# Up projections of the last feed-forward as seven block products instead of eight, in a two-block transformer kernel

## The chip, the cores and the metric

The kernel runs on one core of one Trainium2 chip. The metric is device time in microseconds, median of the runs. TensorE (PE) multiplies matrices: the weights are loaded as the stationary operand (PEld), the activations stream past them, and products accumulate in PSUM, a memory of eight banks of 512 float32 columns, here two tensors `acc` and `sco` of four banks each. VectorE (DVE), ScalarE (ACT) and GpSimd (POOL) do elementwise work; all three reach SBUF, the on-chip memory that holds every other tensor here. SyncE (SP) issues the DMA loads of the weights.

## The reference

Two transformer blocks run one after the other on 512 tokens with 1024 features. The second block adds 16 meta tokens and is feed-forward, attention mixers, feed-forward. Only the last feed-forward changes:

```
def rms_norm(x, g):
    xf = x.astype(jnp.float32)
    y = xf * lax.rsqrt(jnp.mean(xf * xf, axis=-1, keepdims=True) + EPS)
    return (y * g.astype(jnp.float32)).astype(x.dtype)

def swiglu(x, w_in, w_out):
    g, u = jnp.split(x @ w_in, 2, axis=-1)
    return (jax.nn.silu(g) * u) @ w_out

h = h + token_mixer(rms_norm(h, norm_mix[l]), ...)
h = h + 0.5 * swiglu(rms_norm(h, norm_ffn2[l]), w_ffn2_in[l], w_ffn2_out[l])
return rms_norm(h, final_norm)[:, N_META:]
```

`w_ffn2_in` is 1024 x 5632 (gate half and value half of 2816 columns each), `w_ffn2_out` is 2816 x 1024. All inputs are float32.

## The kernel before

Tensors lie transposed: features on the 128 partitions, tokens along the row. A feature axis of 1024 is 8 tiles of 128 rows. Every product is made from two roundings, `x = x_hi + x_lo` and `w = w_hi + w_lo`, each part in the rounded float32 that PE takes in one pass, as three matmuls: `w_hi x_hi + w_hi x_lo + w_lo x_hi`.

The program is a list of phases (`PHASES`). The change touches three of them. `("proj_out", 2)` is the output projection of the mixers, which also adds to `h`, forms `xn_hi` and `xn_lo` (the input of the feed-forward times its gain) and lets POOL sum the squares of `h` for the norm. `("up", 3, 0)` and `("up", 3, 1)` compute gate and value for 11 tiles of hidden features each (22 in all), and `("down", 3, 0)` and `("down", 3, 1)` project those 11 tiles back.

A turn of an up phase makes one tile of hidden features. It is two items: item 0 is the gate tile, item 1 the value tile, in weight slots 0 and 1 (`raw0`, `raw1`). An item is 8 input tiles by 3 matmuls, that is 24 matmuls of 128x512, with its weights handled in two halves of four tiles. For each item SP loads 512 KB in two DMAs, ACT rounds `raw` to `w_hi` (`split_hi`, line 1710), DVE subtracts to `w_lo` (`split_lo`, line 2272) and PE multiplies (`item`, line 1169). Then DVE multiplies the result in PSUM by `rstd` (line 2826), ACT takes the silu (line 2197), DVE multiplies gate by value (line 2862), ACT rounds the product to `hid_hi` (line 2200) and DVE subtracts to `hid_lo` (line 2869). POOL does nothing in these phases. The norm's factor `rstd` comes in the first turn from a matmul of the summed squares (line 1190), a root on ACT and a reciprocal on DVE (line 2811).

Order on each engine is program order. Engines meet through counting semaphores: `n.at(name, k)` is the count that a name has reached after k events of the present turn.

Of the kernel before, what the change touches and what calls it, by code (L numbers as in the profile page):

```python
# [133 lines left out]
UNSCALED = {("proj_out", 1): GAIN["norm_ffn_g"], ("down", 1, 1): N_VEC, ("proj_out", 2): GAIN["norm_ffn2_2"]}  # L134

# [401 lines left out]
def events(phase):  # L537
# [27 lines left out]
    if kind in ("proj_out", "down"):  # L565
        e = {**items(1, 1), **({"sq_ready": 2, "sq_added": 2} if sums_squares(phase) else {})}
        if phase in UNSCALED:
            e.update({"xhi_ready": 2, "xn_ready": 2})
        if phase == ("down", 1, 1):
# [3 lines left out]
        return 4, e  # L573
    if kind == "up":
# [23 lines left out]
class Tally:  # L598
# [19 lines left out]

    def loop(self, first, last, body):
# [29 lines left out]
def build(nc, A, out):  # L649
    with ExitStack() as ctx:  # L650
# [12 lines left out]
        merged = sb("merged", [P, KT, T])  # L663
# [20 lines left out]
        stats = sb("stats", [P, 44])  # L684
        eye, turn_a, turn_b = const[:, 0:P], const[:, P:2 * P], const[0:96, 2 * P:2 * P + 96]
# [39 lines left out]
        meta_tok = flat(probs[:, :, :])[0:META, 0:D]  # L725

# [164 lines left out]
        def _(sp):  # L891
# [90 lines left out]
            for index, ph in enumerate(PHASES):  # L982
# [44 lines left out]
                elif kind == "proj_out":  # L1027
# [4 lines left out]
                    n.loop(1, 4, turn)  # L1032
                elif kind == "up":
# [29 lines left out]
        def _(pool):  # L1063
# [89 lines left out]
        def _(pe):  # L1153
# [25 lines left out]
            def sums(number):  # L1179
# [461 lines left out]
            for index, ph in enumerate(PHASES):  # L1641
# [60 lines left out]
        def _(act):  # L1702
            n = Tally(act)

            def split_hi(slot, k, tiles):

                act.wait_ge(S[f"raw_in{slot}"], n.at(f"raw_in{slot}", 32 * k))
                act.wait_ge(S[f"item_done{slot}"], n.at(f"item_done{slot}", k - 1))
                for a, b, parts in split_parts(tiles):
                    act.activation(w_hi[slot][:, a:b, :], raw[slot][:, a:b, :], ACT.Copy).then_inc(  # L1710
                        S[f"hi_ready{slot}"], parts)

# [359 lines left out]
            for index, ph in enumerate(PHASES):  # L2072
# [137 lines left out]
        def _(dve):  # L2210
# [55 lines left out]
            def split_lo(slot, k, tiles):  # L2266

                done = 2 * k - 2
                for a, b, parts in split_parts(tiles):
# [3 lines left out]
                                      w_hi[slot][:, a:b, :].bitcast(F32), ALU.subtract).then_inc(S[f"split{slot}"], parts)  # L2273

# [456 lines left out]
            for index, ph in enumerate(PHASES):  # L2731
# [31 lines left out]
                elif kind == "resplit":  # L2763
                    c0 = META
                    for k in range(KT):
# [3 lines left out]
                                          ALU.subtract).then_inc(S["xn_ready"], 1)  # L2769
                elif kind in ("proj_out", "down"):  # L2770
# [3 lines left out]
                    def turn(i, tiles=own):  # L2774
                        for s in range(2):
# [129 lines left out]
```

## Time and profile before

| | |
|---|---|
| time, median of 3 runs | 2275.52 us (2275.37 to 2279.98) |
| profiled execution, span from first to last instruction | 2277.5 us |
| PE busy | 2219.2 us (97%) |
| DVE busy | 1243.9 us (55%) |
| ACT busy | 903.5 us (40%) |
| POOL busy | 220.5 us (10%) |
| mean granted clock of PE, share of full speed | 0.995 |

The profiled execution has no time of its own beside its span, which lies 2.0 us above the median of the timed runs and within their range. Busy times are sums over instructions; a busy PE includes overlap of pipelined matmuls.

### The profile page before, as it was taken

To read this page: it belongs to the slowest core of one execution; us is meant where nothing else is said; L and a number is where in the kernel's file an instruction comes from. 1 tells how busy PE (TensorE), PEld (TensorE's weight loads), DVE (VectorE), ACT (ScalarE), POOL (GpSimd) and SP (SyncE) were. 2 spreads that over 40 slices of the span, in tenths; PEclk is the share of its full clock that TensorE was granted. 3 is DMA by queue.
4 is the path that set the end of the run, shared out by engine and by line. 5 is a ranking of instruction groups with operands and counts; after the bars stand their busy time and mean duration, and the time that the engine had idled before them with its cause. 6 is when DMAs were issued, how large, how long until landed. Compare 5 with 4: busy or idle time off the path is not lost.

```text
span 2277.5 us, 36049 instructions
## 1 busy us (share of the span) xinstructions
PE 2219.2 (97%) x12592; PEld 1820.2 (80%) x12592; DVE 1243.9 (55%) x2668; ACT 903.5 (40%) x1815; POOL 220.5 (10%) x201
## 2 busy tenths in 40 slices
PE   8999999999999999999999899999999999999998
PEld 6567766778888889999999777777777787888887
DVE  5779786467736745533442545544555655443442
ACT  5455445444414443322322444444444433322332
POOL 0100043310000031000001000111100130000001
PEclk9999999999999999999999999999999999999999
DMA  4111211235533342342233222243333233332332
GB/s 119 36 37 37 65 47 52 79 102 150 157 102 95 113 129 78 91 129 88 85 106 99 57 85 81 74 111 94 98 92 98 81 97 89 95 108 77 97 105 75
DMA packets 400393, 205.67 MB, mean 90 GB/s; under 512 B 68956, under 2 KB 393928, under 8 KB 400284
## 3 DMA queue, kind: packets, MB, share of 16 engines
q1 hardware_dynamic: 399365, 203.83, 31.3%
q8 instruction: 63, 1.03, 0.2%
q10 hardware_dynamic: 919, 0.43, 0.1%
q14 instruction: 46, 0.38, 0.1%
HBM read 201.94 MB, written 14.80 MB: 95 GB/s over the span
## 4 chain that ended last, share of the span: by engine, by line
PE 64%; issue 19%; DVE 4%; ACT 2%; POOL 1%; POOLq 0%; DVEq 0%; ACTq 0%
PE acc L1169 34%; PE acc L1474 16%; PE acc L1220 5%; PE sco L1509 2%; PE acc L1573 1%; PE acc L1569 1%; DVE w_lo L2272 1%; PE sco L1262 1%; PE sco L1549 1%; POOL vT L1095 1%; PE acc L1309 1%; PE acc L1549 0%; PE sco L1529 0%; PE acc L1296 0%; DVE bias L2260 0%
## 5 line engine op out<-in xcount | busy, mean ns | idle before, releaser
L1710 ACT ACTIVATE w_hi<-raw 128x512 fp32r<-128x512 f32 (+4 forms) x656 | 372.0, 614 | 694.4 <-PE acc L1169 661.2
L2272 DVE TENSOR_TENSOR w_lo<-raw,w_hi 128x512 fp32r<-128x512 f32 (+4 forms) x656 | 423.2, 685 | 143.8 <-ACT w_hi L1710 139.5
L1169 PE MATMUL acc<-xn_hi,w_hi 128*128 128x512 f32 (+1 forms) x1408 | 421.1, 340 | 2.1 <-DVE qbuf L2826 2.1
L1169 PE MATMUL acc<-xn_lo,w_hi 128*128 128x512 f32 (+1 forms) x1408 | 422.1, 340 | 0.0
L1169 PE MATMUL acc<-xn_hi,w_lo 128*128 128x512 f32 (+1 forms) x1408 | 420.3, 339 | 0.0
L1169 PEld LDWEIGHTS acc<-xn_hi,w_hi 128*128 128x128 f32 x1408 | 241.9, 188 | 35.8 <-DVE qbuf L2826 3.0
L1169 PEld LDWEIGHTS acc<-xn_lo,w_hi 128*128 128x128 f32 x1408 | 241.2, 188 | 31.2 <-issue 0.5
L1169 PEld LDWEIGHTS acc<-xn_hi,w_lo 128*128 128x128 f32 x1408 | 241.5, 188 | 30.0
L1169 PE MATMUL acc<-hid_lo,w_hi 128*128 128x512 f32 (+1 forms) x832 | 261.5, 349 | 0.0
L1169 PE MATMUL acc<-hid_hi,w_lo 128*128 128x512 f32 (+1 forms) x832 | 260.6, 348 | 0.0
L1169 PE MATMUL acc<-hid_hi,w_hi 128*128 128x512 f32 (+1 forms) x832 | 259.8, 347 | 0.8 <-DVE hid_lo L2768 0.8
L2826 DVE TENSOR_TENSOR qbuf<-acc,v_tok 128x512 f32<-128x512 f32 (+1 forms) x132 | 91.7, 695 | 249.8 <-PE acc L1169 249.7
L1474 PE MATMUL acc<-xn_hi,w_hi 128*128 128x264 f32 (+1 forms) x576 | 187.7, 367 | 13.2 <-DVE xn_lo L2299 3.8
L2778 DVE SCALAR_TENSOR_TENSOR h<-acc,h 128x512 f32 (+3 forms) x64 | 44.5, 695 | 267.6 <-PE acc L1169 267.6
L1474 PE MATMUL acc<-xn_hi,w_lo 128*128 128x264 f32 (+1 forms) x576 | 172.8, 341 | 0.0
L1474 PE MATMUL acc<-xn_lo,w_hi 128*128 128x264 f32 (+1 forms) x576 | 172.5, 340 | 0.0
L1169 PEld LDWEIGHTS acc<-hid_hi,w_hi 128*128 128x128 f32 x832 | 144.5, 188 | 23.2 <-issue 1.1
L1169 PEld LDWEIGHTS acc<-hid_lo,w_hi 128*128 128x128 f32 x832 | 144.5, 188 | 21.2
L1169 PEld LDWEIGHTS acc<-hid_hi,w_lo 128*128 128x128 f32 x832 | 144.8, 188 | 20.4
L1474 PEld LDWEIGHTS acc<-xn_hi,w_hi 128*128 128x128 f32 x576 | 98.7, 189 | 36.8 <-issue 17.8
L1220 PE MATMUL acc<-xn_hi,w_hi 128*128 128x512 f32 x240 | 118.6, 494 | 0.9 <-DVE w_lo L2272 0.6
L1474 PEld LDWEIGHTS acc<-xn_hi,w_lo 128*128 128x128 f32 x576 | 99.3, 189 | 12.6
(397 smaller groups left out, 3065.7 us busy)
## 6 DMA issues: line engine op xcount, KB each, us to landing
raw<-in_w_ffn_in SPq DMA_DIRECT2D x176, 256.0 KB, 3.0
raw<-in_w_in SPq DMA_DIRECT2D x118, 256.0 KB, 3.2
raw<-in_w_up SPq DMA_DIRECT2D x88, 256.0 KB, 3.0
raw<-in_w_ffn_out SPq DMA_DIRECT2D x32, 384.0 KB, 3.3
raw<-in_w_gate SPq DMA_DIRECT2D x48, 256.0 KB, 3.0
raw<-in_w_ffn_out SPq DMA_DIRECT2D x32, 320.0 KB, 3.7
raw<-in_w_out SPq DMA_DIRECT2D x32, 256.0 KB, 2.8
bias<-grids_dram SPq DMA_DIRECT2D x64, 128.0 KB, 2.9
```

The lines of the kernel that those rows point to most:

```text
L1095: ins = pool.tensor_tensor(square_sum[:, c0:T], square_sum[:, c0:T], probs[:, s, c0:T], ALU.add)
L1169: mm = pe.matmul(acc[0:m, 2 * slot + b, 0:size], w[slot][:, t, 0:m], x[:, place(t), c:c + size], start=(t == 0 and w is w_hi and x is xh), ...
L1220: mm = pe.matmul(acc[0:m, slot, 0:SEQ], w[slot][:, t, 0:m], x[:, t, META:T], start=(t == 0 and w is w_hi and x is xh), stop=(t == tiles - ...
L1262: mm = pe.matmul(sco[:, hh, :], queries_a[i][r, P * (t - 1):P * t], kbuf[r, i // 2, META:T], start=True, stop=True)
L1309: mm = pe.matmul(acc[64 * hh:64 * hh + 64, 3, o:o + P], front_values(u)[:, 1 + b, 0:64], pt[:, hh, 1 + b, :], start=b == 0, stop=b == 3)
L1474: mm = pe.matmul(acc[:, b if wide else slot, 0:size], w[slot][:, t, :], x[:, t, c:c + size], start=(t == 0 and w is w_hi and x is xh), sto ...
L1509: mm = pe.matmul(sco[:, bank, to:to + size], qbuf[r, i % 2, TILES[t][0]:TILES[t][0] + P], kbuf[r, keys_at(name, i), c:c + size], start=Tru ...
L1549: mm = pe.transpose(turned_of[x % 2][:, b * P:(b + 1) * P], prob_of[u % 4][:, real + b * P:real + (b + 1) * P], eye)
L1710: act.activation(w_hi[slot][:, a:b, :], raw[slot][:, a:b, :], ACT.Copy).then_inc(S[f"hi_ready{slot}"], parts)
L2272: dve.tensor_tensor(w_lo[slot][:, a:b, :], raw[slot][:, a:b, :], w_hi[slot][:, a:b, :].bitcast(F32), ALU.subtract).then_inc(S[f"split{slot ...
L2778: dve.scalar_tensor_tensor(out=x, in0=banks(acc, 2 * s, blk), scalar=factor, in1=x, op0=ALU.mult, op1=ALU.add).then_inc(S[f"acc_free{s}"], 1)
L2826: dve.tensor_tensor(span(scaled[s], blk), banks(acc, 2 * s, blk), span(rstd, blk), ALU.mult).then_inc(S[f"acc_free{s}"], 1)
```

## The change

Each turn of the two up phases of the last feed-forward (`PAIRED = (3,)`) becomes one 2x2 block product by the scheme of Strassen and Winograd. The weights of a turn are four blocks of four input tiles each: even and odd input tiles, of the gate (a11, a12) and of the value. The activations are four blocks too: even and odd input tiles, left and right half of the tokens. Seven products of sums of blocks stand for the eight block products that gate and value need. Each product is 4 tiles by 3 matmuls of 128x256, so a turn is 84 matmuls of 256 columns in place of 48 matmuls of 512.

The weight sums `s1` to `s4` are made on POOL from the raw weights (`sum_blocks`), for the turn after the present one. ACT rounds seven blocks in each turn (`block_rounded`) and DVE lowers seven (`block_lowered`), each of 128x512. The sums of activation blocks (`t1` to `t4`) are made once, on POOL, in `("proj_out", 2)` (`feed`), and rounded and lowered there by ACT and DVE (`feed_pairs`).

Products accumulate in four banks of `sco`. Where one partial result serves two outputs, ACT copies it to SBUF (`copies`, in `kbuf`). DVE adds a bank and a copy (`joined`) for three of the four half tiles, POOL adds two copies for the fourth (`join_value`). DVE scales the gate by `rstd` and POOL the value (`scale_value`). Raw weights have two buffers: even turns use `aux`, odd turns `raw0` and `raw1`. The loads of a turn are four DMAs of 256 KB. The proj_out and up phases of this feed-forward are written out straight instead of in loops.

Core of the diff:

```diff
+PAIRED = (3,)
+PRODUCTS = ("a11", "a12", "s2", "s1", "s3", "a22", "s4")
@@ SP
+                    def pair_rows(r):
+                        ...
+                        sp.wait_ge(S["block_split"], n.at("block_split", -7 if r >= 2 else -7 * r))
+                        for s in range(2):
+                            c = (ph[2] * HALF + r) * P + s * D_FF
+                            for first in (0, 4):
+                                sp.dma_start(pair_raw[r % 2][s][:, first:first + 4, :],
+                                             w_up[ph[1]][:, first:first + 4, c:c + P]).then_inc(
+                                                 S[f"{landings(r)[0]}{s}"], 16)
@@ POOL
+            def sum_blocks(r, ahead):
+                ...
+                pool.wait_ge(S["block_split"], max(0, n.at("block_split", 7 * ahead - 3)))
+                pool.tensor_tensor(s_sums["s1"], value[:, 0], value[:, 1], ALU.add).then_inc(S["s_made"], 1)
+                pool.wait_ge(S["s_made"], n.at("s_made", done + 1))
+                pool.tensor_tensor(s_sums["s2"], s_sums["s1"], gate[:, 0], ALU.subtract).then_inc(S["s_made"], 1)
+                pool.tensor_tensor(value[:, 0], gate[:, 0], value[:, 0], ALU.subtract).then_inc(S["s_made"], 1)
+                pool.wait_ge(S["s_made"], n.at("s_made", done + 2))
+                pool.wait_ge(S["block_split"], n.at("block_split", 7 * ahead))
+                pool.tensor_tensor(s_sums["s4"], gate[:, 1], s_sums["s2"], ALU.subtract).then_inc(S["s_made"], 1)
+                    def pool_turn(r):
+                        if r > 0:
+                            scale_value(r - 1)
+                        if r + 1 < HALF:
+                            sum_blocks(r + 1, 1)
+                        join_value(r)
@@ PE
+                banks_of = (0, 1, 0, 2, 0, 3, 2)
+                for b, name in enumerate(PRODUCTS):
+                    pe.wait_ge(S["block_split"], n.of("block_split", r, b + 1))
+                    ...
+                    elif name == "s2":
+                        pe.wait_ge(S["copied"], n.of("copied", r, 1))
+                    elif name == "s1":
+                        pe.wait_ge(S["joined"], n.of("joined", r, 0))
+                    ...
+                    for j in range(4):
+                        ...
+                        for w, x in ((block_hi, x_hi), (block_hi, x_lo), (block_lo, x_hi)):
+                            mm = pe.matmul(sco[:, banks_of[b], 0:half], w[b][:, j, :], x,
+                            ...
@@ ACT
+                block_rounded(6, r, 0)
+                if r > 0:
+                    silu(r - 1)
+                copy(0, 0, 1)
+                next_block(0)
+                if r > 0:
+                    round_hidden(r - 1)
+                next_block(1)
+                copy(1, 0, 3)
+                next_block(2)
+                copy(2, 2, 4)
+                next_block(3)
+                copy(3, 0, 5)
+                next_block(4)
+                ...
+                next_block(5)
@@ DVE
+                if r > 0:
+                    gate_joined(r - 1)
+                    if r == 1 and ph[2] == 0:
+                        dve.wait_ge(S["root_ready"], n.of("root_ready", 0, 1))
+                        dve.reciprocal(rstd[:, first:T], root[:, first:T]).then_inc(S["rstd_ready"], 1)
+                        ...
+                    scale_gate(r - 1)
+                block_lowered(5, r, 0)
+                block_lowered(6, r, 0)
+                if r > 0:
+                    hidden(r - 1)
+                ...
+                dve.tensor_tensor(scaled[0][:, left], bank(1), copies[0][:, 0:half], ALU.add).then_inc(S["joined"], 1)
+                next_block(0)
+                if r > 0:
+                    lower_hidden(r - 1)
+                next_block(1)
+                next_block(2)
+                next_block(3)
+                next_block(4)
+                ...
+                dve.tensor_tensor(scaled[1][:, left], bank(3), copies[3][:, 0:half], ALU.add).then_inc(S["joined"], 1)
```

On DVE, one turn in the middle of the first up phase stands so in the kernel before (the lines 2271, 2856 and 621 are loop bookkeeping):

```order
L2826 TENSOR_TENSOR qbuf<-acc,v_tok 128x512
L2271 ISA
L2272 TENSOR_TENSOR w_lo<-raw,w_hi 128x512
L2271 REGISTER_ALU
L2272 TENSOR_TENSOR w_lo<-raw,w_hi 128x512
L2826 TENSOR_TENSOR qbuf<-acc,v_tok 128x512
L2272 TENSOR_TENSOR w_lo<-raw,w_hi 128x512 x2
L2856 REGISTER_ALU
L2862 TENSOR_TENSOR pt<-vT,qbuf 128x512
L2869 TENSOR_TENSOR hid_lo<-pt,hid_hi 128x512
```

and an even turn so in the changed kernel (`sco` is PSUM, all other names are SBUF; `kbuf` holds the copies, `wx` and `w` the seven rounded blocks):

```order
L2629 TENSOR_TENSOR qbuf<-sco,kbuf 128x256
L2634 TENSOR_TENSOR qbuf<-qbuf,v_tok 128x512
L2613 TENSOR_TENSOR w_lo<-aux,w_hi 128x512 x2
L2641 TENSOR_TENSOR pt<-vT,qbuf 128x512
L2668 TENSOR_TENSOR qbuf<-sco,kbuf 128x256
L2613 TENSOR_TENSOR wx_lo<-raw,wx_hi 128x512
L2647 TENSOR_TENSOR hid_lo<-pt,hid_hi 128x512
L2613 TENSOR_TENSOR wx_lo<-raw,wx_hi 128x512
L2613 TENSOR_TENSOR wx_lo<-aux,wx_hi 128x512
L2613 TENSOR_TENSOR w_lo<-aux,w_hi 128x512
L2613 TENSOR_TENSOR w_lo<-raw,w_hi 128x512
L2678 TENSOR_TENSOR qbuf<-sco,kbuf 128x256
```

A turn goes from 8 DVE instructions, six of them with both inputs in SBUF, to 13, ten of them with both inputs in SBUF.

On POOL, where nothing stood in these phases, a turn is now (two turns shown, the first with its sums from `raw`, the second from `aux`):

```order
L1188 TENSOR_TENSOR qbuf<-qbuf,v_tok 128x512
L1169 TENSOR_TENSOR aux<-raw1 128x512
L1171 TENSOR_TENSOR aux<-aux,raw0 128x512
L1172 TENSOR_TENSOR raw1<-raw0,raw1 128x4x128
L1175 TENSOR_TENSOR aux<-raw0,aux 128x512
L1196 TENSOR_TENSOR qbuf<-kbuf 128x256
L1188 TENSOR_TENSOR qbuf<-qbuf,v_tok 128x512
L1169 TENSOR_TENSOR aux<-aux 128x512
L1171 TENSOR_TENSOR aux<-aux 128x512
L1172 TENSOR_TENSOR aux<-aux 128x4x128
L1175 TENSOR_TENSOR aux<-aux 128x512
L1196 TENSOR_TENSOR qbuf<-kbuf 128x256
```

That is five instructions of 512 columns and one of 256 for each turn, all reading SBUF.

On DVE at the end of the output projection and the first turn of the up phase, the changed kernel has (line 2701 adds an item to `h`, 2613 lowers weight blocks, 2711 and 2696 lower activations and their sums):

```order
L2701 SCALAR_TENSOR_TENSOR h<-acc,h 128x512
L2613 TENSOR_TENSOR wx_lo<-aux,wx_hi 128x512 x3
L2613 TENSOR_TENSOR w_lo<-aux,w_hi 128x512 x2
L2711 TENSOR_TENSOR xn_lo<-qbuf,xn_hi 128x256
L2696 TENSOR_TENSOR xn_lo<-kbuf,xn_hi 128x256
L2701 SCALAR_TENSOR_TENSOR h<-acc,h 128x512
L2711 TENSOR_TENSOR xn_lo<-qbuf,xn_hi 128x512
L2696 TENSOR_TENSOR t_lo<-kbuf,t_hi 128x256 x3
```

Five weight blocks now stand ahead of the lowering of the last two activation tiles.

## Rows read from the trace of the kernel before

**Rows 1.** The page: busy time of each engine, and the chain that ended last
```profile
PE 2219.2 (97%) x12592; PEld 1820.2 (80%) x12592; DVE 1243.9 (55%) x2668; ACT 903.5 (40%) x1815; POOL 220.5 (10%) x201
PE 64%; issue 19%; DVE 4%; ACT 2%; POOL 1%; POOLq 0%; DVEq 0%; ACTq 0%
```

**Rows 2.** Windows: a 264-column phase, then the two last up phases
```profile
core 0: us, PE busy (x) PEld busy (x) DVE busy (x) ACT busy (x) POOL busy (x), PEclk, DMA share, GB/s
1065.33:1182.79 117.46, 117.46 (x962) 117.46 (x961) 52.85 (x80) 34.88 (x60) 0.00 (x0) 1.00 0.32 93
1914.49:2014.57 100.08, 100.08 (x433) 81.14 (x432) 47.12 (x73) 31.15 (x54) 0.00 (x0) 1.00 0.33 97
2092.47:2192.55 100.08, 100.08 (x433) 81.14 (x432) 47.13 (x72) 31.14 (x54) 0.00 (x0) 1.00 0.33 95
```

**Rows 3.** Groups by line, from 1600 us on: one instruction's mean ns
```profile
L2272 DVE TENSOR_TENSOR w_lo<-raw,w_hi 128x512 fp32r<-128x512 f32 x140 | 90.4, 687 | 29.4 <-ACT w_hi L1710 28.7
L2272 DVE TENSOR_TENSOR w_lo<-raw,w_hi 128x256 fp32r<-128x256 f32 x40 | 15.6, 429 | 16.8 <-ACT w_hi L1710 16.8
L1710 ACT ACTIVATE w_hi<-raw 128x512 fp32r<-128x512 f32 x140 | 80.5, 623 | 165.0 <-PE acc L1169 161.3 <-PE acc L1474 3.7
L1710 ACT ACTIVATE w_hi<-raw 128x256 fp32r<-128x256 f32 x40 | 14.3, 408 | 12.0 <-PE acc L1474 12.0
L2826 DVE TENSOR_TENSOR qbuf<-acc,v_tok 128x512 f32<-128x512 f32 x44 | 30.3, 691 | 104.5 <-PE acc L1169 104.5
L2862 DVE TENSOR_TENSOR pt<-vT,qbuf 128x512 f32<-128x512 f32 x22 | 15.0, 683 | 0.0
L2197 ACT ACTIVATE vT<-qbuf 128x512 f32<-128x512 f32 x22 | 13.6, 617 | 2.8 <-DVE qbuf L2826 2.8
```

**Rows 4.** Timeline of POOL (start, duration; both in us)
```profile
1426.24 1.50 POOL L1143 TENSOR_TENSOR bias<-bias,const 128x512 f32<-128x512 f32 x1
1435.99 1.09 POOL L1143 TENSOR_TENSOR bias<-bias,const 128x512 f32<-128x512 f32 x1
1701.32 1.29 POOL L1149 TENSOR_TENSOR merged<-merged,bias 128x512 f32<-128x512 f32 x1 [61.50 <-DVE small L2572]
1828.75 1.75 POOL L1149 TENSOR_TENSOR merged<-merged,bias 128x512 f32<-128x512 f32 x1 [9.82 <-DVE small L2572]
1845.51 2.27 POOL L1149 TENSOR_TENSOR merged<-merged,aux 128x512 f32<-128x512 f32 x1 [1.04 <-DVE small L2572]
1863.97 1.36 POOL L1095 TENSOR_TENSOR vT<-vT,probs 128x512 f32<-128x512 f32 x1 [4.87 <-ACT probs L2139]
```

**Rows 5.** Timeline of DVE around the same moments
```profile
1426.11 2.18 DVE L2272 TENSOR_TENSOR w_lo<-raw,w_hi 128x512 fp32r<-128x512 f32 x2
1701.28 0.50 DVE L2601 CUSTOM_DVE_ANT_0 aux<-sco,bias,small 128x272 f32<-128x272 f32 x1
1828.60 0.74 DVE L2272 TENSOR_TENSOR w_lo<-raw,w_hi 128x256 fp32r<-128x256 f32 x2
1845.36 1.27 DVE L2272 TENSOR_TENSOR w_lo<-raw,w_hi 128x512 fp32r<-128x512 f32 x2
1857.34 1.28 DVE L2272 TENSOR_TENSOR w_lo<-raw,w_hi 128x512 fp32r<-128x512 f32 x2
1859.09 0.75 DVE L2785 SCALAR_TENSOR_TENSOR xn_lo<-h,gains,xn_hi  x1 [0.46 <-ACT xn_hi L2147]
1864.68 1.20 DVE L2785 SCALAR_TENSOR_TENSOR xn_lo<-h,gains,xn_hi  x1 [0.50 <-ACT xn_hi L2147]
```

**Rows 6.** Timelines at the start of the up phase, DVE then PE
```profile
1904.45 3.35 DVE L2811 RECIPROCAL v_tok<-vT 128x512 f32<-128x512 f32 x1 [1.31 <-ACT vT L2177]
1907.84 1.29 DVE L2826 TENSOR_TENSOR qbuf<-acc,v_tok 128x512 f32<-128x512 f32 x2
...
1908.59 0.50 PE L1169 MATMUL acc<-xn_hi,w_hi 128*128 128x512 f32 x1 [1.07 <-DVE qbuf L2826]
```

**Rows 7.** The page's DMA issues: KB each, us to landing
```profile
raw<-in_w_ffn_in SPq DMA_DIRECT2D x176, 256.0 KB, 3.0
```

**Rows 8.** Windows (columns as in the second group): the first 60 us
```profile
0.00:60.00 60.00, 50.61 (x231) 38.84 (x231) 36.95 (x72) 32.83 (x61) 4.93 (x14) 0.91 0.43 119
```

More of the change, by code:

```diff
@@ L573, in events @@
         return 4, e
+    if paired(phase):
+        return HALF, {"s_made": 4, "block_hi": 7, "block_split": 7, "product": 7,
+                      "copied": 4, "joined": 3, "value_half": 1, "gate_scaled": 1, "value_scaled": 1, "hid_hi": 1, "hid_ready": 1,
+                      "silu_ready": 1, "hid_ready_f32": 1}
     if kind == "up":
@@ L617, in at, with of @@
         return self.turn * self.each.get(event, 0) + (self.before.get(event, 0) + k)
+    def of(self, event, turn, k):
+        return self.before.get(event, 0) + turn * self.each.get(event, 0) + k
     def loop(self, first, last, body):
@@ L1073, in _ @@
                 pool.memset(raw[s][:, :, :], 0.0).then_inc(fills, 1)
+            def sum_blocks(r, ahead):
+                done = 4 * ahead
+                gate, value = (even_odd(x) for x in pair_raw[r % 2])
+                kind, landed = landings(r)
+                for s in range(2):
+                    pool.wait_ge(S[f"{kind}{s}"], n.at(f"{kind}{s}", landed))
+                pool.wait_ge(S["block_split"], max(0, n.at("block_split", 7 * ahead - 3)))
[6 more added lines that the diff above has]
+                pool.tensor_tensor(s_sums["s4"], gate[:, 1], s_sums["s2"], ALU.subtract).then_inc(S["s_made"], 1)
@@ L1074, in _, with scale_value, join_value @@
             for index, ph in enumerate(PHASES):
                 n.enter(index)
-                if sums_squares(ph):
+                if paired(ph):
+                    first, last = (META, T) if columns_of(ph) == 1 else (0, T)
+                    def scale_value(r):
+                        pool.wait_ge(S["joined"], n.of("joined", r, 2))
+                        pool.wait_ge(S["value_half"], n.of("value_half", r, 1))
+                        if r == 0:
+                            pool.wait_ge(S["rstd_ready"], n.of("rstd_ready", 0, 1 if ph[2] == 0 else 0))
+                        pool.tensor_tensor(scaled[1][:, first:last], scaled[1][:, first:last], rstd[:, first:last],
+                                           ALU.mult).then_inc(S["value_scaled"], 1)
+                    def join_value(r):
+                        half = (T - first) // 2
+                        pool.wait_ge(S["copied"], n.of("copied", r, 4))
+                        pool.wait_ge(S["hid_ready_f32"], n.of("hid_ready_f32", r, 0))
+                        pool.tensor_tensor(scaled[1][:, first + half:T], copies[2][:, 0:half], copies[3][:, 0:half],
+                                           ALU.add).then_inc(S["value_half"], 1)
+                    def pool_turn(r):
[4 more added lines that the diff above has]
+                        join_value(r)
+                    for r in range(HALF):
+                        n.straight(r, pool_turn)
+                    scale_value(HALF - 1)
@@ L1672, in _ @@
                     final()
+                elif paired(ph):
+                    for r in range(HALF):
+                        n.straight(r, lambda i: pairs(ph, i))
                 elif kind in ("proj_out", "up", "down"):
@@ L1711, in split_hi, with block_rounded @@
                         S[f"hi_ready{slot}"], parts)
+            def block_rounded(j, r, ahead):
+                (kind, landed), name = landings(r), PRODUCTS[j]
+                if name in ("a11", "a12"):
+                    act.wait_ge(S[f"{kind}0"], n.at(f"{kind}0", landed))
+                elif name == "a22":
+                    act.wait_ge(S[f"{kind}1"], n.at(f"{kind}1", landed))
+                else:
+                    act.wait_ge(S["s_made"], n.at("s_made", 4 * ahead + {"s1": 1, "s2": 2, "s3": 3, "s4": 4}[name]))
+                act.activation(block_hi[j], block_source(name, r), ACT.Copy).then_inc(S["block_hi"], 1)
@@ L2774, in turn @@
                     def turn(i, tiles=own):
+                        if tiles == (0, 0) and index + 1 < len(PHASES) and paired(PHASES[index + 1]):
+                            for j in range(5):
+                                block_lowered(j, 0, 0)
                         for s in range(2):
```

273 lines of the change are left out of this document (267 added, 6 removed).

## The prediction

> **What bounds the kernel now.** The page comes first: PE is busy 97% of the span, the chain that ended last is mostly PE and issue, and POOL is busy 10% [rows 1]. Then the windows over the two up phases: 100.08 us hold 18 items of 24 matmuls, all of it PE busy at full clock, DVE busy 47.12, ACT 31.15, POOL 0 [rows 2]. So an item takes 100.08 / 18 = 5.56 us, a turn of two items 11.12 us, the 22 turns 244.6 us. Nothing but PE matters there. Last the groups and the timelines of DVE and POOL, for what the added instructions cost. The runs' median is 2275.5 us and the profiled span 2277.5; I add the sum to the span and take 2 us off at the end.
>
> **What PE gains.** 48 matmuls of 512 columns become 84 of 256. A 512-column matmul takes 5.56 / 24 = 231.7 ns. The 264-column phase has 962 in 117.46 us, 122.1 ns each, with its weight loads busy without a gap [rows 2]. A line through both gives 0.442 ns a column and 5.4 ns, so 118.6 ns at 256 columns: 84 x 118.6 = 9.96 us a turn. If the weight load is what holds 264 columns at 122.1, it is 10.26. I take 9.96. If PE stayed the bound: 22 x (11.12 - 9.96) = 25.5 us gained.
>
> **What ACT and the loads cost: nothing.** ACT gets seven roundings, 0.62 each, four copies of 256 columns at 0.41, silu 0.62, and a hidden rounding like it [rows 3]: 7.2 us under a turn of 10 or more. Loads stay 1 MB a turn in 256 KB pieces, 3.0 us to landing [rows 7]; a raw buffer is free after the seventh block of turn r-2, a quarter into that turn, and is read a turn later, some 8 us. Uncovered, a late load would delay `s1` and all behind it.
>
> **What DVE and POOL cost by themselves.** DVE has ten instructions of 512 columns and three of 256 with one input in PSUM. At 0.69 and 0.43 [rows 3] that is 8.2 us, back to back less (a pair takes 1.28, so the second adds 0.60 [rows 5]). POOL has five of 512 and one of 256: an undisturbed one takes 1.29 [rows 4], half for the small one, 7.1 us. Each alone fits under 9.96.
>
> **But not side by side.** This is the step that decides. The rows pair up in time:
> - DVE lowers two blocks from 1845.36 to 1846.63 [rows 5]. POOL's sum starts at 1845.51 and ends at 1847.78, 2.27 us against 1.29 undisturbed, 1.15 after DVE ends [rows 4]. At 1828.75 it takes 1.75 and ends 1.16 after DVE.
> - The other way: DVE's `xn_lo` takes 0.75 at 1859.09, and 1.20 at 1864.68 under POOL's 1863.97 to 1865.33; it ends 0.55 after POOL [rows 4, 5].
> - At 1426 both meet: DVE's pair takes 2.18 for 1.28, POOL 1.50 for 1.09.
> - A DVE instruction with one input in PSUM and one in SBUF, at 1701.28, leaves POOL's at 1.29.
>
> So a DVE instruction with two SBUF inputs and a POOL one that reads SBUF hardly overlap. The Trainium skill, "SBUF — State Buffer", section "Who interferes with whom", has this rule: DVE's second SBUF input goes through a read interface that GpSimd shares, and the later one fully blocks. The direction agrees with the rows; its size is a rival below.
>
> Ten of DVE's thirteen and all six of POOL's are of that kind. The floor of a turn is then 10 x 0.60 + 5 x 1.15 + 0.60 (the small one: bounds 0.58 from half of 1.15 and 0.65 from half of 1.29) = 12.35 us, above PE's 9.96 and above the 11.12 of today. Bounds: if the sums, whose inputs are strided, run like the mask addition (1.09 alone; 1426 to 1428.29 is 2.18 for three instructions, so 2.18 - 1.20 = 0.98 for POOL's), four of them at 0.98 give 11.65. If each handover costs what an undisturbed start does, 10 x 0.69 + 5 x 1.29 + 0.65 = 14.0.
>
> **Does the order fill it?** I laid out one turn. DVE's gate join runs beside POOL's `scale_value`; then scaling, two lowerings and `hidden` run as a train while POOL's `s1` stands; `s1` goes in the left join's place; lowering 0, `lower_hidden` and lowering 1 run; now DVE has nothing until `s2` is summed and rounded, so POOL runs `s2` and `s3`; then lowering 2 and 3, POOL's `s4` while ACT rounds `s3`, lowering 4, the value join, with `join_value` behind it. The interface is in use nearly all the time and the layout closes at 12.45. PE's seven products have two and a half us of slack in it: `s2` waits for copy 0, that for the silu, that for the scaled gate. I take **12.5** (nearer 12.35 than 14.0, since DVE's instructions come in trains and an alternation ends 0.55, not 0.69, after POOL).
>
> **The edges.** Turn 0 has no scaling or hidden work (seven lowerings and five POOL instructions, 9.4 us on the interface, with waits 10.5). Turn 10 has no sums and no next blocks: PE's 9.96, with the wait for the gate 10.3. Its tail (join, scale, silu, hidden, roundings, some 5 us) is hidden by down's first item, which reads the last hidden tile after 10 tiles of 3 matmuls, 6.95 us. A phase is 10.5 + 9 x 12.5 + 10.3 = 133.3 us against 122.3: +11.0, twice is +22.0.
>
> At the start of the first phase, let E be the end of the last output item. POOL reaches `sum_blocks(0)` only behind the activation sums and squares of the item pair before, about E - 4.5, so `s1` to `s3` end near E - 0.6. The lowering of blocks 2 to 4 stands ahead of tile 6 of the activations on ACT and DVE, that ahead of tile 7. PE wants tile 6 at E + 1.1 and gets it at about E + 2; it wants tile 7 at about E + 3.4 and gets it near E + 5.8, since `h`, scaling, rounding, lowering (about 0.69 each) follow behind the sum `t1`. That is +3.4, with the shared interface +4. In turn 1 the reciprocal, 3.35 us [rows 6], stands between the gate join and its scaling, and `scale_value`, first in POOL's turn, waits for it too: +3.35, less the 1.07 that it costs PE today [rows 6]: +2.3. In the output projection itself DVE's and POOL's shared time is about 9.2 of 11.12: nothing.
>
> Sum: 22.0 + 4 + 2.3 = +28. 2277.5 + 28 = 2305.5, less 2: **2304 us**.
>
> **Rivals.**
> - **A, the forecast:** DVE and POOL share, a turn is 12 to 13.7. Rows 4 and 5 for it. 18 inner turns x (12.0 to 13.7): 2295 to 2326. Chance 0.78.
> - **B, PE stays the bound (faster):** the lowerings and sums overlap after all, because their inputs differ from those in the trace. It decides once shared time a turn falls below 9.96; parity is at 10.9 (28 / 18 = 1.6 below 12.5). 2277.5 - 25.5 + 6.3, less 2: 2256. Against it: even the low bound is 11.65, and each row above shows the stretch. 0.08. The Trainium skill ("TensorE: Matmul & The Clock Gate") states N / 2.4 GHz and about 2.5 ns start to start when warm, 109 ns at 256 columns, an estimate from that page; the trace does not agree at 264 (122.1), and it would help this rival alone, by 84 x 22 x 9.4 ns = 17 us.
> - **C, shared but cheap:** POOL's strided sums hold the interface for 0.9 or less, 11 us a turn: 2272 to 2284. 0.06.
> - **D, full exclusion at full durations:** each instruction holds the interface for its whole undisturbed time, 14.0 a turn (the page "SBUF — State Buffer" says "for the full instruction"). 18 x 1.5 = +27: 2331. For it: nothing can start early. Against it: 1.15 and 0.55 after a handover are below 1.29 and 0.69. 0.06.
> - **E, the clock:** the first 60 us, with PE busy 50.6, ran at 0.91 of full clock [rows 8]. If PE, idle a fifth of each turn, were granted 1.2 GHz, a turn would be near 20 us: above 2430. The idle time comes in pieces of a few hundred ns to 2 us. 0.02.
>
> **How the numbers follow.** 2304 is A's middle. The range 2286 to 2330 holds A with all of its own width and the nearer parts of C and D, with B, E and the ends of C and D left out. No change means within 0.2%, 4.6 us, about what a measurement of this kernel can tell. Faster: B and a little of C, 0.09. Same: most of C, 0.05. Slower: A, D, E, 0.86.
>
> **What would show it.** In the windows of the up phases PE is no longer busy throughout, its matmuls of 256 columns are about 119 ns apart within a product, and a turn repeats every 12 to 13 us. POOL's instructions there average 1.6 us or more, not 1.29, and the lowerings on DVE 0.8 or more, not 0.69; POOL and DVE together are busy nearly throughout. In the waits, PE waits for `copied` or block lowerings, and ACT and DVE for POOL's sums. The reciprocal's turn is some 3 us longer. I am wrong if POOL's instructions keep 1.29 beside DVE's lowerings, or if a turn repeats every 10 us.

## The result, and the profile after

The changed kernel takes 2318.7 us (median of 5 runs, 2315.0 to 2319.3), the kernel before beside it 2277.1 us (median of 5 runs, 2275.4 to 2280.0 but for a single one of 3680.7, which the ratio leaves out). The ratio is 1.018, 95% interval 1.0166 to 1.0192: slower, on the side that was forecast, and 14.7 us above the 2304 us predicted. The profiled execution took 2315.0 us, its span 2313.0 us.

The page of the changed kernel, its busy times and its chain, in the form of [rows 1]:

```profile
PE 2205.0 (95%) x13384; PEld 1848.9 (80%) x13384; DVE 1388.6 (60%) x2794; ACT 977.8 (42%) x1993; POOL 423.6 (18%) x349
PE 58%; issue 21%; DVE 8%; ACT 3%; POOL 1%; ACTq 0%; POOLq 0%; DVEq 0%
```

Over the span PE is still busy 95%, and that says nothing: the loss lies in an eighth of the span. The windows show it (columns as in [rows 2]): the same 100 us as there, then three single turns, each from one gate join on DVE (line 2629) to the next, then ten microseconds of the start.

```profile
1914.49:2014.57 100.08, 81.03 (x623) 79.29 (x624) 91.20 (x100) 48.35 (x100) 68.42 (x47) 0.94 0.30 85
...
1939.39:1953.48 14.09, 11.70 (x86) 11.53 (x85) 11.72 (x13) 6.32 (x14) 8.97 (x7) 0.88 0.27 77
1953.48:1965.77 12.29, 10.43 (x86) 10.07 (x85) 11.54 (x14) 6.33 (x14) 7.92 (x7) 1.00 0.30 86
1965.77:1978.35 12.58, 10.17 (x86) 9.99 (x85) 11.85 (x13) 6.33 (x13) 8.92 (x7) 1.00 0.29 85
...
1894.00:1904.00 10.00, 6.53 (x29) 5.97 (x29) 7.66 (x9) 6.43 (x13) 8.60 (x8) 0.50 0.05 14
```

PE was busy for all of the 100.08 us before and is for 81.03 now; DVE went from 47 to 91, POOL from 0 to 68. Each phase has 11 turns, 0 to 10. The 17 inner turns are 2 to 9 of the first phase and 1 to 9 of the second (turn 1 of the first holds the reciprocal).
The groups of DVE and POOL from 1895 us on (one instruction's mean ns behind the busy time). They answer to the 687 ns in [rows 3] and the 1.29 us in [rows 4]:

```profile
L2613 DVE TENSOR_TENSOR w_lo<-aux,w_hi 128x512 fp32r<-128x512 f32 x66 | 77.6, 1192 | 7.3 <-ACT w_hi L1933 6.1
L2641 DVE TENSOR_TENSOR pt<-vT,qbuf 128x512 f32<-128x512 f32 x22 | 28.1, 1276 | 1.4 <-ACT vT L1977 1.4
L1188 POOL TENSOR_TENSOR qbuf<-qbuf,v_tok 128x512 f32<-128x512 f32 x22 | 29.8, 1356 | 28.4 <-DVE qbuf L2678 22.3 <-DVE v_tok L2659 6.1
L1169 POOL TENSOR_TENSOR aux<-aux 128x512 f32<-128x512 f32 x11 | 16.8, 1523 | 41.2 <-issue 41.2
L1172 POOL TENSOR_TENSOR aux<-aux 128x512 f32<-128x512 f32 x11 | 18.6, 1691 | 0.0
```

DVE's timeline inside the third of those turns (start, duration), and POOL's:

```profile
1967.05 1.78 DVE L2613 TENSOR_TENSOR w_lo<-raw,w_hi 128x512 fp32r<-128x512 f32 x1
1968.75 1.78 DVE L2613 TENSOR_TENSOR w_lo<-aux,w_hi 128x512 fp32r<-128x512 f32 x1
1970.44 1.77 DVE L2641 TENSOR_TENSOR pt<-vT,qbuf 128x512 f32<-128x512 f32 x1
...
1974.42 1.28 DVE L2613 TENSOR_TENSOR wx_lo<-aux,wx_hi 128x512 fp32r<-128x512 f32 x2
```

```profile
1968.35 1.62 POOL L1171 TENSOR_TENSOR aux<-aux 128x512 f32<-128x512 f32 x1
1969.93 1.73 POOL L1172 TENSOR_TENSOR aux<-aux 128x512 f32<-128x512 f32 x1
1971.63 1.72 POOL L1175 TENSOR_TENSOR aux<-aux 128x512 f32<-128x512 f32 x1
1975.96 0.94 POOL L1196 TENSOR_TENSOR qbuf<-kbuf 128x256 f32<-128x256 f32 x1 [2.61 <-ACT kbuf L1957]
```

While both have work they take turns, one instruction of each every 1.70 us, and the record of each covers its own time and the other's. When POOL stands still (1974.42), a pair on DVE is back to 1.28 us.

Last the waits from 1895 us on (us in total, times, longest), and PE's three waits in the first turn:

```profile
ACT hid_hi L1982 <- DVE pt L2641: 61.2, 20, 3.7
...
PE sco L1392 <- ACT kbuf L1957: 42.6, 25, 2.7
```

```profile
1893.04 0.39 PE L1392 MATMUL sco<-xn_hi,wx_hi 128*128 128x256 f32 x1 [3.25 <-DVE xn_lo L2711]
1896.10 0.58 PE L1392 MATMUL sco<-xn_hi,wx_hi 128*128 128x256 f32 x1 [0.71 <-DVE xn_lo L2711]
1899.87 0.55 PE L1392 MATMUL sco<-t_hi,wx_hi 128*128 128x256 f32 x1 [2.76 <-issue]
```

In a turn, ACT rounds the hidden tile (line 1982) when DVE has formed it (line 2641), copy 1 stands behind that rounding on ACT, and PE's `s3` waits for copy 1, 1.4 us in six of the inner turns and 2.2 to 2.4 us in eleven.

### The profile page after: what moved, and what is told of

Read it like the earlier page. It is cut to its first block, busy times and chain, and to the rows that moved or that the text cites. A ratio compares the mean times of both kernels' runs of the same rounds, so it can differ in the third digit from the quotient of the medians.

```text
span 2313.0 us, 37903 instructions
## 1 busy us (share of the span) xinstructions
PE 2205.0 (95%) x13384; PEld 1848.9 (80%) x13384; DVE 1388.6 (60%) x2794; ACT 977.8 (42%) x1993; POOL 423.6 (18%) x349
## 4 chain that ended last, share of the span: by engine, by line
PE 58%; issue 21%; DVE 8%; ACT 3%; POOL 1%; ACTq 0%; POOLq 0%; DVEq 0%
PE acc L1338 23%; PE acc L1682 15%; PE sco L1392 6%; PE acc L1428 5%; DVE w_lo L2613 2%; PE sco L1717 2%; PE acc L1781 1%; DVE pt L2641 1%; PE acc L1777 1%; DVE w_lo L2607 1%; PE sco L1470 1%; PE sco L1757 1%; POOL vT L1264 1%; PE acc L1517 1%; PE acc L1757 1%
## 5 line engine op out<-in xcount | busy, mean ns | idle before, releaser
L1921 ACT ACTIVATE w_hi<-raw 128x512 fp32r<-128x512 f32 (+4 forms) x560 | 315.3, 610 | 525.8 <-PE acc L1338 492.7
L2607 DVE TENSOR_TENSOR w_lo<-raw,w_hi 128x512 fp32r<-128x512 f32 (+4 forms) x568 | 369.3, 690 | 137.0 <-ACT w_hi L1921 133.8
L1338 PE MATMUL acc<-xn_hi,w_hi 128*128 128x264 f32 (+1 forms) x1056 | 281.2, 320 | 1.1 <-DVE qbuf L3276 1.1
L1338 PE MATMUL acc<-xn_hi,w_lo 128*128 128x264 f32 (+1 forms) x1056 | 282.2, 322 | 0.0
L1338 PE MATMUL acc<-xn_lo,w_hi 128*128 128x264 f32 (+1 forms) x1056 | 281.9, 321 | 0.0
L1682 PE MATMUL acc<-xn_hi,w_hi 128*128 128x264 f32 (+1 forms) x576 | 187.3, 366 | 13.2 <-DVE xn_lo L2740 3.8
L1338 PEld LDWEIGHTS acc<-xn_hi,w_hi 128*128 128x128 f32 x1056 | 176.1, 188 | 18.1 <-DVE qbuf L3276 1.5
L1338 PEld LDWEIGHTS acc<-xn_hi,w_lo 128*128 128x128 f32 x1056 | 175.6, 188 | 15.0
L1338 PEld LDWEIGHTS acc<-xn_lo,w_hi 128*128 128x128 f32 x1056 | 174.6, 188 | 15.6 <-issue 0.2
L3228 DVE SCALAR_TENSOR_TENSOR h<-acc,h 128x512 f32 (+3 forms) x56 | 39.0, 696 | 239.6 <-PE acc L1338 239.6
L1682 PE MATMUL acc<-xn_hi,w_lo 128*128 128x264 f32 (+1 forms) x576 | 172.1, 339 | 0.0
L1682 PE MATMUL acc<-xn_lo,w_hi 128*128 128x264 f32 (+1 forms) x576 | 172.0, 339 | 0.0
L1338 PEld LDWEIGHTS acc<-hid_lo,w_hi 128*128 128x128 f32 x832 | 144.4, 188 | 21.2
L3276 DVE TENSOR_TENSOR qbuf<-acc,v_tok 128x512 f32<-128x512 f32 (+1 forms) x88 | 61.4, 698 | 143.8 <-PE acc L1338 143.7
L1682 PEld LDWEIGHTS acc<-xn_hi,w_hi 128*128 128x128 f32 x576 | 98.3, 188 | 36.7 <-issue 17.8
L1682 PEld LDWEIGHTS acc<-xn_hi,w_lo 128*128 128x128 f32 x576 | 98.8, 188 | 12.6
```

The source lines that it names most:

```text
L1338: mm = pe.matmul(acc[0:m, 2 * slot + b, 0:size], w[slot][:, t, 0:m], x[:, place(t), c:c + size], start=(t == 0 and w is w_hi and x is xh), ...
L1682: mm = pe.matmul(acc[:, b if wide else slot, 0:size], w[slot][:, t, :], x[:, t, c:c + size], start=(t == 0 and w is w_hi and x is xh), sto ...
L2607: dve.tensor_tensor(w_lo[slot][:, a:b, :], raw[slot][:, a:b, :], w_hi[slot][:, a:b, :].bitcast(F32), ALU.subtract).then_inc(S[f"split{slot ...
L3228: dve.scalar_tensor_tensor(out=x, in0=banks(acc, 2 * s, blk), scalar=factor, in1=x, op0=ALU.mult, op1=ALU.add).then_inc(S[f"acc_free{s}"], 1)
L3276: dve.tensor_tensor(span(scaled[s], blk), banks(acc, 2 * s, blk), span(rstd, blk), ALU.mult).then_inc(S[f"acc_free{s}"], 1)
```

## The experiments

Two theories at the start. Theory 1, the forecast: DVE's instructions with two SBUF inputs and POOL's that read SBUF exclude each other, and the sum of their times is the turn. Theory 2: POOL's own time with its chain of sums makes the turn, whatever DVE does. The runs share their runs of the kernel before, 2276.3 to 2276.4 us. In all, "join" is the first gate join, counted from the end of the last output item (5.56 us behind the addition of the item before).

**e1, e2: the sums away, or writes in their place.** The four weight sums become fills of 16 columns (e1), or two fills of 128x512 each (e2, one in a phase's first turn); `s1` to `s4` are not computed.

```diff
-pool.tensor_tensor(s_sums["s1"], value[:, 0], value[:, 1], ALU.add)
+pool.memset(s_sums["s1"][:, 0, 0:16], 0.0)                                    # e1
+pool.memset(probs[:, 0, 0:512], 0.0); pool.memset(s_sums["s1"], 0.0)          # e2
```

> The four weight sums of a turn on POOL are replaced by four fills of 128x16 in the same place and with the same waits, so s1 to s4 are left out of the computation. Shared-interface theory (a DVE instruction with two SBUF inputs and a POOL one that reads SBUF exclude each other, and a turn of 12.3 to 12.6 us is made of that): only scale_value and join_value are left on POOL, shared time falls to about 7.8 us a turn, PE binds at 10.0 to 10.4, no turn shows a lowered clock, DVE's lowerings fall to 0.69. Time 2318.7 - 22 x 2.6, less some us at the start: 2250 to 2265. Rival, order (PE waits on a chain of in-order ACT and DVE work, whatever POOL does): turns stay at 12 or more, 2300 to 2318. Rival, POOL's own time: the same as the shared-interface theory here; the next kernel tells them apart.

> The four weight sums of a turn are replaced by two fills each of 128x512, about 1.1 us a sum by the fills of the profile (0.53 us for 528 columns), which write SBUF and read nothing; s1 to s4 are left out of the computation. POOL is busy nearly as long as before. Shared-interface theory, by its read side: as the kernel with short fills, 2252 to 2270, DVE's lowerings at 0.69. Rival, POOL's own time (the sums come late because POOL is slow, not because it is blocked or blocks): within 10 us of the changed kernel less 22 x 0.2 to 0.5, 2305 to 2318. Rival, the exclusion covers writes too: turns of 12, DVE's lowerings over 0.69, 2300 to 2318.

e1: 2262.1 us, ratio 0.9935 (0.9918 to 0.9951). e2: 2260.4 us, 0.9927 (0.9905 to 0.9949). Inner turns are 9.95 us in both, PE's own time. The groups of e2:

```profile
L2621 DVE TENSOR_TENSOR w_lo<-aux,w_hi 128x512 fp32r<-128x512 f32 x66 | 46.1, 714 | 28.5 <-ACT w_hi L1941 28.5
...
L1183 POOL MEMSET aux<- 128x512 f32 x21 | 11.2, 531 | 0.0
```

Eight fills keep POOL busy 4.2 us a turn, and DVE's lowering takes 714 ns, 713 in e1, 1192 in the changed kernel. So it is not that POOL works but that it reads. Theory 2 falls: POOL is busy 5.9 us a turn in e2, where the prediction had put its work at 7.1 undisturbed, so that the fills are shorter by 1.2 us, but the turn fell by 2.5. The Trainium skill, "SBUF — State Buffer", section "Who interferes with whom", says that a VectorE instruction with two SBUF inputs contends with a GpSimd one that reads SBUF and not with one that only writes; these two runs agree.

**e5: the sums on DVE.** POOL keeps the scaling of the value and the fourth join.

```diff
 block_lowered(6, r, 0)
+next_sum(1)
+next_sum(2)
 ...
 next_block(0)
+next_sum(3)
 ...
 next_block(1)
+next_sum(4)
```

> The four weight sums of a turn run on DVE, between the lowerings; POOL keeps scale_value and join_value. The full result is computed. Shared-interface theory: a sum costs 0.60 on DVE in place of 1.15 on POOL, shared time 14 x 0.60 + 1.75 = 10.2, with DVE's three joins 10.6 to 11.1 a turn; 20 turns x 1.9 less than now and a shorter start: 2265 to 2285, near the kernel before. Rival, DVE's own work is the bound (busy 11.5 of 12.3 us a turn now): four more instructions make a turn 14.5 or more, 2355 or above. Rival, order: 2310 to 2330.

2279.1 us, 1.0016 (1.0007 to 1.0026), inner turns 10.87 but for one of 10.43. As theory 1 expected: a sum takes 0.68 us on DVE, and the engine that already had the most work, with 14 such instructions, does them in a shorter turn than the two engines together (12.5, e4 below).

**e3, e4: the long turns.** e3 puts eight matmuls that nobody reads (1.9 us) ahead of `s3`'s wait; e4 moves the hidden tile's rounding behind copy 1 and its lowering behind block 1.

```diff
+for _ in range(8):                                              # e3, PE, r > 0
+    pe.matmul(acc[:, 0, :], xn_hi[:, 0, 0:P], xn_hi[:, 0, 0:512], start=True, stop=True)
 pe.wait_ge(S["copied"], n.of("copied", r, 2))
```

```diff
 copy(0, 0, 1)                                                   # e4, ACT
 next_block(0)
-if r > 0:
-    round_hidden(r - 1)
 next_block(1)
 copy(1, 0, 3)
+if r > 0:
+    round_hidden(r - 1)
```

> Eight matmuls of 128x512 into an unused bank, 1.85 us at full clock, stand in each turn from the second on ahead of product s3's wait for copy 1, where PE sits idle for 1.4 or 2.4 us. Clock theory (the turns of 14 us, seven of twenty, are those in which PE is granted 1.2 GHz for a while, because it idles there): those turns vanish, -12 us, and the fillers cost 0.4 where the idle time is 1.4 only, +4: 2308 to 2312. If the long turns have another cause and the low clock follows from them, they stay, and the time is 2318 to 2326.

> The changed kernel with two instructions moved: in every turn ScalarE rounds the hidden tile behind copy 1 instead of ahead of it, and VectorE lowers it behind block 1 instead of ahead of it. The work is the same. Theory, the shared interface: the ten VectorE and six GpSimd instructions of a turn take the same 12.3 us whatever PE's wait for copy 1 does, so turns stay at 12.2 to 12.6 us; PE's idle piece of 2.4 us ahead of s3 gets shorter, and some of the 14.1 us turns may go with it: 2303 to 2318 us. Rival, the order: the chain hidden, rounding of hidden, copy 1, s3 is what makes the turn long, so it falls to 11.5 us or less: below 2300 us.

e3: 2315.9 us (1.0177), inner turns 12.6, apart from one of 12.35 and one of 13.16, none of 14.1. e4: 2313.6 us (1.0159), inner turns 12.4 to 12.8, and one of 11.8. Windows of one turn of e3, then of three of e4:

```profile
1955.22:1967.84 12.62, 12.05 (x94) 11.37 (x93) 12.05 (x13) 6.33 (x13) 9.04 (x7) 1.00 0.29 85
```

```profile
1956.11:1968.65 12.54, 10.15 (x73) 9.97 (x72) 12.51 (x14) 6.41 (x13) 8.90 (x6) 0.86 0.29 84
1968.65:1981.25 12.60, 11.74 (x99) 11.56 (x98) 12.56 (x15) 6.27 (x14) 9.17 (x6) 1.00 0.29 85
1981.25:1993.82 12.57, 10.16 (x86) 9.98 (x85) 12.54 (x14) 6.23 (x13) 9.15 (x6) 1.00 0.30 85
```

e4 came out as the shared reads had it (2303 to 2318 us, 15 of the 17 inner turns within 12.2 to 12.6), and the order alone is not the bound. e3 missed its 2308 to 2312: the long turns went, as the clock theory said, but the short ones grew from 12.3 to 12.6, and the last turn of each phase, where nothing waits, grew by the fillers, from 11.57 to 13.4 us. e4 says more. The clock still falls to 0.86, in a turn in which PE waits 2.39 us for copy 1, and the turn is no longer: DVE is busy 12.51 of 12.54 us, so the turn is the shared reads and nothing else. In the changed kernel the chain of the hidden tile left DVE 11.7 us of work in a turn of 14.1, and there the slow matmuls showed. So the 14.1 needs both, the fall and an order that lets it through; e3 takes away the one, e4 the other. The 17 inner turns add up to 220.8 us in the changed kernel, 214.8 in e3 and 212.9 in e4. Part of that is lost again in the last turn of each phase, 11.57 us in the changed kernel; in e4 it takes 12.04 and 13.57, the second with the clock at 0.87 and DVE busy only 7.8 us. From the last output item to the end of the program e3 is 3.4 us shorter than the changed kernel and e4 6.8, their medians 2.8 and 5.1.

**e6: the control**, `PAIRED = ()` in the changed program.

> The changed program with its pair scheme switched off (PAIRED is empty): eight block products, no weight sums, the phases in loops as before. It shows whether anything else in the changed file (memory layout, the new names) has a part. Theory: nothing else has, 2276 us within 0.2% (2272 to 2281). Rival, a part of the loss comes from elsewhere in the file: above 2285 us.

2276.0 us, 0.9996 (0.9987 to 1.0005). Nothing but the scheme makes the difference.

**e7, e10, e12: the start.** e7 and e10 put only blocks 0 and 1 ahead of activation tiles 6 and 7; e10 also puts copy 0 of the first turn ahead of blocks 4 to 6. e12 is the changed kernel with matmuls in PE's waits.

```diff
 elif s == 0:                                                    # e7, e10: ACT (DVE alike)
-    first_blocks(0, 5)
+    first_blocks(0, 2)
 ...
+if i == 3 and k == 2:
+    first_blocks(2, 3)
```

```diff
+if name == "s2" and r == 0 and ph[2] == 0:                      # e12: 12 ahead of tile 6, 11 here
+    fill(11)
 pe.wait_ge(S["block_split"], n.of("block_split", r, b + 1))
```

> The changed kernel with the work at the end of the output projection reordered and nothing else: before activation tiles 6 and 7 only the two blocks that the first products need are rounded and lowered (block 2 behind tile 7, blocks 3 and 4 at the end), and GpSimd makes s1 and s2 behind t1, s3 and s4 behind the last squares. Theory: the start costs 6 to 7 us in stalls (3.25, 0.71 and 2.76 us in the changed kernel) and clock, because the five weight blocks stand ahead of the activations: the first gate join comes 14 to 17 us after the last output item, not 21.2, and the time falls by 4 to 7 us to 2311 to 2315. Rival, the chain from the last output item to tile 7 (add, scaling, t2, rounding, lowering, each with its wait) sets the start: the join stays at 20 to 21 us, the time within 2 us of the changed kernel's. The turns stay as they are.

> The start order once more, on the changed kernel and nothing else. The first attempt moved five weight blocks behind the activations and left copy 0 of the first turn behind blocks 3 to 6, so PE waited 7.05 us for it in one piece where the changed kernel had waited 6.7 in three. Now copy 0 stands ahead of block 4, and GpSimd makes s3 and s4 ahead of the last squares. Theory, the order of the start: s2 begins 5.4 us after the last output item, when block 2 is lowered, and the first gate join comes 14 to 17 us after it, not 21.2: 2311 to 2315 us. Rival: PE comes to the turn in a drained state whatever the order, the granted clock falls to one half for 8 us as before and eats the gain: join at 19 us or more, 2316 us or more.

> The changed kernel, with products that nobody reads in PE's two long waits of the first turn: 12 matmuls of 128x512 (2.8 us) into a bank not yet in use ahead of activation tile 6, and 11 (2.5 us) ahead of s2. They fit in the waits of 3.25 and 2.76 us. Theory, the clock's share of the start: the granted clock was 0.50 from 1894 to 1904 us, and the 29 matmuls recorded there lay 0.21 us apart, not 0.118. With PE kept busy the clock stays at 1.00; 29 by 0.095 is at most 2.8 us: the first gate join comes 18.5 to 20 us after the last output item instead of 21.2, and the time is 1 to 3 us below the changed kernel's 2318.7. Rival, the chain of VectorE and ScalarE sets the start and the half clock lies in its shade: the join stays at 21 us, the time within 1 us.

| run | us | join, us | PE's waits in the first turn, us |
|---|---|---|---|
| changed | 2318.7 | 21.2 | 3.25, 0.71, 2.76 |
| e7 | 2319.7 | 21.2 | 0.88, 7.05 |
| e10 | 2318.1 | 19.8 | 0.86, 4.75 |
| e12 | 2319.0 | 20.5 | 0.56, 1.36, 0.65 beside the filling |

All three missed what they were expected to give. e7 (14 to 17 us for the join) failed by my own order: copy 0 stood on ACT behind blocks that wait for POOL's `s3`. In e10 (again 14 to 17) two lowerings of `t` on DVE, alone 0.75 us, took 2.89 beside the sums that had been moved next to them, and copy 0 waits for them. Each order moved the wait elsewhere. The clock was not the main cause either; the windows of e12, where the changed kernel had 0.50:

```profile
1894.00:1898.00 4.00, 3.44 (x19) 2.66 (x18) 3.91 (x5) 1.97 (x5) 2.95 (x3) 1.00 0.00 0
1898.00:1902.00 4.00, 2.64 (x17) 2.19 (x16) 2.28 (x4) 2.60 (x6) 3.21 (x4) 1.00 0.01 2
```

At full clock in the first turn, the join comes 0.7 us sooner, not 1.2 to 2.7, and the time is the same. The next turn is 1.1 us shorter too, but the clock fell in seven of e12's inner turns, not six, and they take 222.7 us, 1.9 more.

**e8, e9, e11: a faster version.** e8 is e5 with the orders of e4 and e7, the sums of the first turn back on POOL. e9 takes POOL out of the turns (the fourth join reads bank 0 of PSUM and copy 2, and PE's next `a11` waits for it) with the start of e10. e11 is e9 with 18 matmuls in the wait for copy 0.

```diff
+def scale_value(turn):                                          # e9, on DVE
+    dve.tensor_tensor(scaled[1][:, first:T], scaled[1][:, first:T], rstd[:, first:T], ALU.mult)
+def join_value(turn):
+    dve.tensor_tensor(scaled[1][:, right], bank(0), copies[2][:, 0:half], ALU.add)
```

> An attempt to do better than both kernels: the sums of all turns but the first on VectorE, the hidden tile's rounding and lowering behind copy 1 and block 1, and the start order of the run before this one. Theory: with the sums on VectorE a turn took 10.87 us, 0.6 of it PE's wait for copy 1; without that wait VectorE's own work sets it, 14 instructions of 0.60 to 0.68 and three of 0.42, 10.2 to 10.5 us a turn; 18 turns by 0.5 and the start's 5 us off 2279 give 2263 to 2270 us. Rival, GpSimd's two instructions still hold VectorE's up wherever they stand: turns of 10.8 us, 2274 us or more.

> The same start, and in the turns no GpSimd at all: sums, scaling of the value and the fourth join on VectorE, the join out of PSUM bank 0 and copy 2. VectorE then has 15 instructions of 512 columns at 0.60 and four of 256 at 0.34: 10.4 us a turn. With GpSimd's last two instructions on the side the turn was 10.92, VectorE busy throughout. Theory: an instruction on GpSimd costs VectorE more (1.1 and some 0.3 us) than doing the work itself (0.60 and 0.34), so turns fall to 10.3 to 10.6; 18 turns by 0.45 and what the start gives (0 to 6 us) off 2280 give 2266 to 2273 us, the first version below the kernel before. Rival, VectorE pays no more for GpSimd's two than their own work would cost it: 10.9 or more a turn, 2276 us or more.

> The version with no GpSimd in the turns (2272.3 us), with 18 such matmuls (4.2 us) in PE's wait of 4.7 us ahead of s2. There the clock fell to 0.50 from 1902 to 1906 and 0.67 to 1910. Theory: 42 matmuls are recorded in those 8 us, some 30 of them 0.095 us late, 2.8 us; the first join comes 17 to 18.5 us after the last output item, not 19.7, and the time is 2269 to 2271 us, 0.995 to 0.9975 of the kernel before. Rival: VectorE, which is busy without a gap from 1899 to 1912 us, sets the first turn, and nothing is gained: 2272 to 2273 us.

e8 missed its 2263 to 2270 and came out as its rival had it: 2279.9 us, 1.0019 (1.0010 to 1.0028). e9: 2272.3 us, 0.9980 (0.9971 to 0.9989). e11 missed its 2269 to 2271: 2273.5 us, 0.9989 (0.9980 to 0.9998), its join at 18.1 us, not 19.7, with nothing to show in the time. Two turns of e8, then three of e9:

```profile
1949.70:1971.60 21.90, 21.55 (x183) 21.37 (x182) 21.76 (x35) 13.47 (x27) 6.98 (x5) 1.00 0.34 97
```

```profile
1938.48:1970.30 31.82, 30.53 (x253) 30.00 (x254) 31.61 (x59) 19.55 (x39) 0.00 (x0) 1.00 0.35 100
```

DVE is busy throughout in both. In these two of e8 a turn is 10.95 us (10.85 on the mean of its inner turns), though its 14 instructions at 0.60 and three at 0.34 make 9.4. In e9 it does POOL's work itself, 10.4 by the same prices, and needs 10.61, at the edge of the 10.3 to 10.6 expected. That sum is thus 0.2 short, and POOL's two cost DVE 1.2 to 1.3 us a turn where their work costs 0.94. e9 and e11, which have these turns, are the only full versions below the kernel before, by 0.2% and 0.1%.

## Why the prediction was right

The time lies inside the range, but partly by luck: the range was laid out for the price of the shared reads, and what moved the time up were the start and the clock.

- **PE's gain: right.** Turns of 9.95 us in e1 and e2, forecast 9.96; those two lie 14 and 16 us below the kernel before, and PE is the bound there.
- **The step that decides, exclusion: right.** e2 and e5 show it, and e1 and e9 agree. Rivals B and C are out: sharing was neither absent nor cheap.
- **The size, 12.5 a turn: right for the shared reads, not for the turn.** The floor from [rows 4] and [rows 5] was 12.35; e4, where DVE has no gap, has 17 turns in 212.9 us, 12.52 each. Rival D, 14.0, took every instruction at its full duration; the page "SBUF — State Buffer" of the Trainium skill, section "SBUF: two separate sides", lets the one that comes second wait for the whole of the first. The runs show the wait, at a lower price: a pair costs 1.70, not 0.69 + 1.29 = 1.98, and a turn 12.52. That DVE's instructions come in trains was wrong while POOL has work queued: the two alternate one by one. It did little harm, since the rows gave nearly the same price for either, 0.60 in a train and 0.55 behind POOL, and 1.15 + 0.55 is 1.70.
- **Mis-sized: the inner turns' clock.** Rival E, put at 0.02, came in part: not every turn at 1.2 GHz but six of the 17 inner turns with a part of them there (0.88 on the mean). With forecast 212.5 us (17 x 12.5) and 220.8 measured it is +8.3 us; e4 gives 7.9 of them back in those turns, and loses 2.5 in the last turn of the two phases.
- **Mis-sized: the start, +4.** The first turn was to take 10.5 us, and with the 4 of the start the join was due at 14.5; it came at 21.2, +6.7. Tile 6 was due at 2 us and came at 4.2, since `t1` stood on POOL behind four sums of 1.3 to 1.7 us; tile 7 at 7.3 and not 5.8; then copy 0 stood on ACT behind roundings and blocks 5 and 6, a queue I had not written out. The clock had 0.7 of it (e12). With the sums away, in e1, the join comes at 16.7 us and PE's wait for tile 6 is gone, so 4.5 of the 6.7 go with POOL's sums, the first turn's and those for the second beside it. No full version brought the join below 18.1. How the rest divides among the queues is not settled.
- **The reciprocal's turn:** 17.13 for 15.85, +1.3. It is 16.1 in e3 and e4, where the clock stays up, but also in e10 and e12, where it falls to 0.89; and in e3 and e4 the turn behind it is longer, so that the two together take 29.3 and 28.9 us against 29.4. The clock has at most 0.6 of it; the rest is open.
- **Sum.** From the end of the last output item to the end, the profile before has 382.0 us and the one after 424.2: +42.2, where +28 was forecast. Of the 14.2 between them 6.7, 1.3 and 8.3 are named; -2.1 I can't place. Ahead of that point the two profiled executions differ by 6.8 us, the one after being shorter, which is why the spans differ by less than the medians (35.5 against 41.6 us).

## What to carry to other kernels

Before moving elementwise work to GpSimd, count the VectorE instructions beside it that read two tensors from SBUF: 0.60 us for each of theirs and 1.15 for each of GpSimd's, per 512 float32 columns, go one behind the other. If VectorE has the time, the same work on VectorE is cheaper than on GpSimd. And where engines of nearly equal load meet, write out every queue of the first turn, not only of the steady one: the first turn cost 6.7 us more than forecast, and two other orders of it gave back 1.4 at most.

## What the runs showed that I had not expected

- The clock fell to one half for a part of six inner turns of the changed kernel. In each of them PE waited 2.4 us in one piece; five others with a wait of 2.2 to 2.4 us, and the six with 1.4, kept the full clock. What decides between them is not settled. In e3 (waits filled) and in the inner turns of e9 (PE busy 30.5 of 31.8 us) it did not fall.
- A fall of the clock cost 0.2 us at most in the inner turns of e4, where DVE has next to no gap, and about 1.5 us a turn where the order let it onto the path: 14.1 against 12.6 us in the changed kernel, 13.57 against 12.04 in the last turns of e4's two phases.
- VectorE and GpSimd, both with work queued, alternate one by one, 1.70 us a pair, less than the two undisturbed durations together (1.98).
